# A chunked scan's running sums repeated over the rows by TensorE products, in place of a store to HBM and broadcast loads

## The chip, the cores and the metric

The kernel runs on one core of a Trainium2 chip. A core has five instruction queues: TensorE (PE, matrix products into PSUM), VectorE (DVE), ScalarE (ACT), GpSimd (POOL) and SyncE (SP); SP and POOL issue the DMAs, which 16 DMA engines carry out. The metric is the device time of one execution in microseconds (us), lower is better.

## What is computed

One layer of a hybrid encoder on 1024 rows of width 1024. After a norm and an input projection come three mixers (a window attention "a", a Mamba-2 scan "b", a banded attention "c"), an output projection, a retrieval of 128 experts per row ("PEER": for each row and each of 128 picks, one row of `peer_u` and one of `peer_v`, 4 KB each, chosen by the data), and a gate. The change is inside the scan:

```python
da_cs = jnp.cumsum(dt * a, axis=2)                              # running sums within a chunk, per head
seg = da_cs[:, :, :, None, :] - da_cs[:, :, None, :, :]         # cs[l] - cs[s] for all pairs
decay = jnp.exp(jnp.where(causal, seg, -jnp.inf))
cb = jnp.einsum("bclhn,bcshn->bclsh", cm, bm) * decay
y_diag = jnp.einsum("bclsh,bcshp->bclhp", cb, xdt)
...
ue = jnp.take(expert_u, it, axis=0)                             # PEER, 128 picks per row
ve = jnp.take(expert_v, it, axis=0)
act = jax.nn.gelu(jnp.einsum("td,ted->te", xt, ue), approximate=False) * gt
return jnp.einsum("te,ted->td", act, ve)
```

## The kernel before

**Tiles and groups.** The 1024 rows are 8 tiles of 128 rows (`TILES`), two tiles to a group (`GT = 2`), so 4 groups. The "front" of a group (`front_steps`) is the norm, the projections, the three mixers, the output projection and the second norm; then come the query products of PEER.

**Slots.** PEER runs as 1024 slots and a tail. Slot n gathers one `peer_u` row per token of a tile (POOL, L868, 512 KB) and takes its dot product on DVE (L1575); 44 slots later (`BEHIND`) the matching `peer_v` rows are gathered (L880, 512 KB) and multiplied on PE (L2017). `u_ring` has 6 places and `v_ring` 8: POOL waits for DVE's dots and for PE's products before it gathers into a place again. The front of group 0 runs before the slots (`before_slots`), the fronts of groups 1, 2 and 3 beside them.

**The order.** Every engine runs the same list of steps in order (`whole_program`), each taking its own part of each step. `beside_slots` spreads the steps of a front over the slots 22 to 204, 204 to 456 and 456 to 708 in proportion to the costs in `PACE`; a step without an entry counts 0.2. PSUM has 8 banks; `plan_banks` gives each step the free bank that was used longest ago, out of 8 at first, and out of 4 from slot 25 on, when the other four hold PEER's sums and its normalised rows. PE waits, before it fills a bank, for the copies out of it.

**The scan.** Once per group, step `cs` makes the running sums of 2 tiles x 16 heads: a product with a triangle of ones `tri` gives `cs` with rows on partitions (L1890), a second one gives them transposed (L1891), ACT copies that to `csT` (L1046), and SP stores it to HBM (`cs_rows`, L809, 16 KB). Per tile come, in the order of `scan_steps`: `b_seg`, two `b_turn` (PE transposes L1898, DVE L1440 and L1441), `b_cb` (PE L1904 and L1906, ACT L1083, DVE L1446), two `b_off` (PE L1918, DVE L1454 to L1466), two `b_diag` (PE L1925, DVE L1471), two `b_state` (PE L1932, DVE L1477). In `b_seg`, SP waits until `seg`, which shares memory with the normalised input `uT`, is free (for tile t, the products of `b_diag` of tile t-1, or `z` for a group's first tile) and loads the 16 x 128 running sums of the tile to all 128 partitions (`seg_rows`, L746, 1 MB). ACT makes relu(cs[s] - cs[l]) head by head (L1076, 16 instructions) and one exp over the tile (L1079). DVE's product L1460 in `b_off` needs that exp; ACT's L1083, which DVE's L1446 needs, stands behind it on ACT.

## Time and profile before

| what | us |
|---|---|
| median of 3 runs | 3769.55 |
| lowest, highest | 3768.69, 3770.98 |
| the profiled execution, its own time | 3753.05 |
| its span | 3751.3 |
| PE, DVE, POOL, ACT busy in the span | 2475.1, 2232.2, 1964.5, 765.6 |

The profile is of one execution. Its span runs from the first to the last instruction, and 1.75 us lie around it. An engine counts as busy while it computes, and POOL's rows are the time to issue a gather. The DMA rows say how busy the 16 DMA engines were and what they moved. A wait names the engine and line that waited, and what ended the wait. All engines are well short of 100%, so the shares alone tell no bound; the stretches have to be read one by one.

### The profile page before, as it was taken

How to read it: one execution, taken by the hardware profiler on the slowest of the kernel's cores; microseconds unless marked ns; L12 is line 12 of the kernel's file. 1: busy time of each engine (PE TensorE's matmuls, PEld its weight loads, DVE VectorE, ACT ScalarE, POOL GpSimd, SP SyncE). 2: the span in 40 equal slices, each digit the busy share in tenths (PEclk: the TensorE clock that was granted, in tenths of full speed). 3: DMA queues.
4: the chain of work that ended last, by engine and by line, in shares of the span. 5: the costliest groups of instructions: out<-in, count | busy, mean ns of one | idle time of the engine just before them, and what ended most of it. 6: DMA issues, size and time to landing. Idle time of an engine off the chain costs nothing. (4 is left out here: it accounts for less than half of the span.)

```text
span 3751.3 us, 33795 instructions
## 1 busy us (share of the span) xinstructions
PE 2475.1 (66%) x10840; PEld 1198.8 (32%) x10840; DVE 2232.2 (60%) x5446; ACT 765.6 (20%) x1750; POOL 1964.5 (52%) x2064
## 2 busy tenths in 40 slices
PE   8869688777777758666777767677725534443554
PEld 5644345443333434322333434322301101110111
DVE  2330868566556766675556766776556666666640
ACT  2331222231112222321122222311111111011010
POOL 0000455545555656555555656655656666666663
PEclk9879899778888777778888877778867666766778
DMA  7325899989999999999999999999999999999995
GB/s 229 114 74 188 317 398 385 352 315 355 406 405 404 376 346 390 384 350 406 405 405 403 369 364 384 382 377 407 401 376 381 372 387 382 378 385 377 367 377 202
DMA packets 427462, 1320.09 MB, mean 352 GB/s; under 512 B 54280, under 2 KB 75920, under 8 KB 425112
## 3 DMA queue, kind: packets, MB, share of 16 engines
q0 software_dynamic: 294912, 1073.87, 74.1%
q1 hardware_dynamic: 132376, 244.06, 17.9%
q8 instruction: 89, 1.46, 0.2%
q14 instruction: 85, 0.70, 0.0%
HBM read 1290.69 MB, written 32.60 MB: 353 GB/s over the span
## 5 line engine op out<-in xcount | busy, mean ns | idle before, releaser
L1575 DVE CUSTOM_DVE_ANT_0 u_ring<-u_ring,ps 128x1024 f32<-128x1024 f32 x1024 | 1231.7, 1217 | 551.4 <-DMA u_ring<-peer_u,idx_u 454.5
L868 POOL DMA_INDIRECT u_ring<-peer_u,idx_u x1024 | 981.5, 958 | 960.6 <-DVE idx_u L1553 379.8
L880 POOL DMA_INDIRECT v_ring<-peer_v,idx_v x1024 | 978.4, 955 | 787.1 <-PE ps L2017 340.4
L2017 PE MATMUL ps<-v_ring,spread 128*32 128x512 f32 x4096 | 752.7, 864 | 851.3 <-DMA v_ring<-peer_v,idx_v 744.2
L2017 PEld LDWEIGHTS ps<-v_ring,spread 128*32 128x32 f32 x4096 | 150.8, 138 | 1233.1 <-issue 1231.0
L1754 PE MATMUL ps<-front 128*128 128x512 f32 x1024 | 458.5, 604 | 2.1 <-ACT front L1117 2.1
L1754 PEld LDWEIGHTS ps<-front 128*128 128x128 f32 x1024 | 194.7, 194 | 271.5 <-issue 271.1
L1950 PE MATMUL ps<-front 128*128 128x512 f32 x512 | 232.8, 613 | 13.6 <-DVE front L1491 8.4
L1873 PE MATMUL ps<-front 128*128 128x256 f32 x768 | 197.8, 415 | 1.4 <-issue 1.4
L1873 PEld LDWEIGHTS ps<-front 128*128 128x128 f32 x768 | 156.1, 209 | 58.1 <-issue 34.6
L1950 PEld LDWEIGHTS ps<-front 128*128 128x128 f32 x512 | 98.9, 197 | 151.6 <-issue 151.6
L1382 DVE CUSTOM_DVE_ANT_0 front<-ps,front 128x640 f32<-128x640 f32 (+2 forms) x64 | 42.1, 658 | 154.2 <-PE ps L1841 59.0
L2047 PE MATMUL ps<-front 128*128 128x512 f32 x256 | 123.7, 637 | 13.9 <-issue 10.6
L1404 DVE SCALAR_TENSOR_TENSOR front<-front,taps 128x256 f32<-128x256 f32 x144 | 69.8, 485 | 100.0 <-ACT hist L1026 59.4
L1938 PE MATMUL ps<-front 128*128 128x512 f32 x256 | 120.8, 627 | 1.9 <-issue 1.9
L1841 PE MATMUL ps<-front 64*128 64x128 f32 x480 | 83.9, 328 | 31.9 <-DVE front L1375 9.8
L1851 PE MATMUL ps<-ident,front 128*128 128x128 f32 x240 | 49.0, 334 | 78.5 <-ACT front L1010 68.9
L1865 PE MATMUL ps<-front 128*128 128x64 f32 x480 | 76.7, 305 | 19.0 <-issue 18.6
L1841 PEld LDWEIGHTS ps<-front 64*128 64x128 f32 x480 | 72.1, 228 | 51.4 <-issue 40.0
L1149 ACT ACTIVATE dots<-dots 128x32 f32<-128x32 f32 x32 | 7.3, 229 | 396.9 <-DVE dots L1575 282.9
L1575 DVE DVE_READ_ACCUMULATOR2_ANT dots<- 128x1 f32 x1024 | 84.5, 83 | 0.0
L1865 PEld LDWEIGHTS ps<-front 128*128 128x128 f32 x480 | 70.2, 220 | 39.3 <-issue 36.4
(232 smaller groups left out, 2725.9 us busy)
## 6 DMA issues: line engine op xcount, KB each, us to landing
front<-w_in SPq DMA_DIRECT2D x76, 1024.0 KB
front<-w_out SPq DMA_DIRECT2D x32, 1024.0 KB
front<-peer_w_query SPq DMA_DIRECT2D x32, 1024.0 KB
u_ring<-peer_u,idx_u POOLq DMA_INDIRECT x1024
v_ring<-peer_v,idx_v POOLq DMA_INDIRECT x1024
front<-c_bias_all SPq DMA_DIRECT2D x32, 320.0 KB
front<-x SPq DMA_DIRECT2D x16, 512.0 KB
front<-cs_rows SPq DMA_DIRECT2D x8, 1024.0 KB
```

What stands on the lines that cost most here:

```text
L868: nc.gpsimd.indirect_dma_start(k.u_ring[:, n % RU, :], None, io["peer_u"][0], bass.IndirectOffsetOnAxis(ap=k.idx_u[:, t % 2, j:j + 1], axi ...
L880: nc.gpsimd.indirect_dma_start(row, None, io["peer_v"][0], bass.IndirectOffsetOnAxis(ap=k.idx_v[:, m % 2, column:column + 1], axis=0)).the ...
L1404: ins = stt(a, k.raw[:, c % 2, j:j + NG], k.taps[:, c, j:j + 1], a, ALU.mult, ALU.add)
L1575: nc.vector.tensor_tensor_reduce(out=row, in0=row, in1=k.un_ps, scale=1.0, scalar=0.0, op0=ALU.mult, op1=ALU.add, accum_out=k.dots[:, t % ...
L1754: last = mm(ps, k.uT[:, half * WCH + c, cols(t)], w[:, c, :], start=(half == 0 and c == 0), stop=(half == 1 and c == WCH - 1))
L1841: last = mm(ps[:, n * P:(n + 1) * P], k.qT_c[side, i // 2, cols(t)], k.kT_c[side, i // 2, kt % 6, :], start=True, stop=True)
L1865: last = mm(ps[:, at:at + HD], k.pT[:, no % 2, j, :], k.v_c[:, kt % 6, i * HD:(i + 1) * HD], start=(kt == c_keys(t)[0]), stop=(kt == t))
L1873: last = mm(ps[:, 0:NG], w[j // WCH][:, j % WCH, c % 4 * P:(c % 4 + 1) * P], k.uT[:, j, :], start=(j == 0), stop=(j == DCH - 1))
L1938: last = mm(ps, k.uT[:, c, cols(t)], w[c // WCH][:, c % WCH, :], start=(c == 0), stop=(c == DCH - 1))
L1950: last = mm(ps, k.yT[:, k.o_chunks[part] + j, cols(t)], w[:, j, :], start=(part == 0 and j == 0), stop=(part == 3 and j == WCH - 1))
L2017: last = mm(k.acc_ps[32 * j:32 * j + 32, half * 512:(half + 1) * 512], centres[:, at:at + 32], row[:, half * 512:(half + 1) * 512], start= ...
L2047: last = mm(ps[:, half * 512:(half + 1) * 512], k.fT[:, c, :], k.wg[:, c, half * 512:(half + 1) * 512], start=(c == 0), stop=(c == DCH - 1))
```

## The change

The running sums get to all partitions by products. For each head, PE multiplies the head's column of `dtA` (128 values, repeated 128 times along the free axis by an access pattern of step 0, as the stationary operand) by `tri`; each of the 128 rows of the result is the head's running sum. Four heads fill one PSUM bank, so a tile has 4 such steps (`b_seg` with `part` 0 to 3) with 16 products in all, and ACT's relu reads PSUM in place of SBUF. The second product of `cs`, its copy, the store of `cs_rows` and the eight 1 MB loads go. ACT now makes the waits that SP made before it overwrote `seg`. `b_seg` gets 1.5 in `PACE` for each part, and takes banks in `plan_banks`.

```diff
+SEG = 4
...
-        out += [("b_seg", t)] + halves("b_turn") + [("b_cb", t)] + halves("b_off") + halves("b_diag") + halves("b_state")
+        out += [("b_seg", t, part) for part in range(B_HEADS // SEG)] + halves("b_turn") + [("b_cb", t)] + halves("b_off") + halves("b_diag") + halves("b_state")
...
-            dt=1.8, cs=0.4, z=4.7, y_n=3.0, b_turn=1.2, b_cb=1.0, b_off=0.6, b_diag=3.5, b_state=0.6, y_t=1.2, b_n=4.0, o=4.7, n2=4.0,
+            dt=1.8, cs=0.4, b_seg=1.5, z=4.7, y_n=3.0, b_turn=1.2, b_cb=1.0, b_off=0.6, b_diag=3.5, b_state=0.6, y_t=1.2, b_n=4.0, o=4.7, n2=4.0,
...
-    singles = dict(n1_t=1, sub=1, a_k=GT, a_turn=1, c_turn=1, a_t=1, c_u=1, x=3, z=1, dt=1, cs=5, b_turn=2, b_cb=2, b_off=1, b_diag=1,
+    singles = dict(n1_t=1, sub=1, a_k=GT, a_turn=1, c_turn=1, a_t=1, c_u=1, x=3, z=1, dt=1, cs=4, b_seg=1, b_turn=2, b_cb=2, b_off=1, b_diag=1,
...
-    def seg_rows(t):
-        g, lt = divmod(t, GT)
-        sp.wait_ge(k.cs_out, 16 * (g + 1))
-        filled(("b_diag", t - 1, 1) if lt else ("z", t + GT - 1, 1))
-        src = k.cs_rows[t * B_HEADS:(t + 1) * B_HEADS, :].rearrange("h l -> (h l)")
-        sp.dma_start(k.seg.rearrange("p h l -> p (h l)"), src.partition_broadcast(P)).then_inc(k.seg_in, 16)
...
-        elif kind == "cs":
-            copied(step)
-            sp.dma_start(k.cs_rows[at[0] * GT * B_HEADS:(at[0] + 1) * GT * B_HEADS, :], k.csT[:]).then_inc(k.cs_out, 16)
-        elif kind == "b_seg":
-            seg_rows(*at)
...
-        if g:
-            act.wait_ge(k.cs_out, 16 * g)
         act_fn(k.cs[:], ps[:, 0:n], ACT.Copy).then_inc(copied_, 1)
-        act_fn(k.csT[:], ps[0:n, P:2 * P], ACT.Copy).then_inc(copied_, 1)
...
-    def b_seg(t):
-        act.wait_ge(k.seg_in, 16 * (t + 1))
-        lt = t % GT
-        for hd in range(B_HEADS):
-            at = lt * B_HEADS + hd
-            last = act_fn(k.seg[:, hd, :], k.seg[:, hd, :], ACT.Relu, bias=k.cs[:, at:at + 1], scale=-1.0)
-        last.then_inc(k.seg_rel, 1)
-        act.wait_ge(k.seg_rel, t + 1)
-        act_fn(k.seg, k.seg, ACT.Exp, scale=-1.0).then_inc(k.seg_exp, 1)
+    def b_seg(t, part):
+        _, ps, copied_ = filled(("b_seg", t, part))
+        if part == 0:
+            last = ("b_diag", t - 1, 1) if t % GT else ("z", t + GT - 1, 1)
+            act.wait_ge(k.filled[k.bank[last].place], k.bank[last].n + 1)
+            if t % GT:
+                act.wait_ge(k.m_full, t * B_GROUPS)
+        for i in range(SEG):
+            hd = part * SEG + i
+            at = t % GT * B_HEADS + hd
+            rel = act_fn(k.seg[:, hd, :], ps[:, i * P:(i + 1) * P], ACT.Relu, bias=k.cs[:, at:at + 1], scale=-1.0)
+        rel.then_inc(copied_, 1)
+        if part == B_HEADS // SEG - 1:
+            act.wait_ge(copied_, k.bank["b_seg", t, part].done)
+            act_fn(k.seg, k.seg, ACT.Exp, scale=-1.0).then_inc(k.seg_exp, 1)
...
-        mm(ps[0:n, P:2 * P], k.dtA[:], k.tri[:], start=True, stop=True)
         mm(ps[:, 2 * P:2 * P + n], k.ones[:], k.dtA[:], start=True, stop=True).then_inc(filled, 1)
+
+    def b_seg(t, part):
+
+        pe.wait_ge(k.dtA_full, t // GT + 1)
+        ps, filled = open_(("b_seg", t, part))
+        for i in range(SEG):
+            at = t % GT * B_HEADS + part * SEG + i
+            last = mm(ps[:, i * P:(i + 1) * P], k.dtA[:, at:at + 1].broadcast_to([P, P]), k.tri[:], start=True, stop=True)
+        last.then_inc(filled, 1)
```

The dispatch of PE calls the new `b_seg`. The line numbers of the kernel after are 1 to 13 off those of before.

On PE, in group 0, tile 0 and the start of tile 1, before (L1831 is `y_t`, L1925 `b_diag`, L1932 `b_state`):

```order
L1831 MATMUL ps<-ident,front 128x128 x16
L1898 MATMUL ps<-ident,front 128x128 x8
L1904 MATMUL ps<-ident,front 128x128 x2
L1906 MATMUL ps<-front 128x128 x2
L1918 MATMUL ps<-state,front 128x512 x2
L1925 MATMUL ps<-front 128x64 x16
L1932 MATMUL ps<-front 128x512 x2
L1898 MATMUL ps<-ident,front 128x128 x8
```

The same place after, where L1890 is the new product:

```order
L1822 MATMUL ps<-ident,front 128x128 x16
L1890 MATMUL ps<-tri,dtA 128x128 x16
L1897 MATMUL ps<-ident,front 128x128 x8
L1903 MATMUL ps<-ident,front 128x128 x2
L1905 MATMUL ps<-front 128x128 x2
L1917 MATMUL ps<-state,front 128x512 x2
L1924 MATMUL ps<-front 128x64 x16
L1931 MATMUL ps<-front 128x512 x2
L1890 MATMUL ps<-tri,dtA 128x128 x16
L1897 MATMUL ps<-ident,front 128x128 x8
```

Sixteen products stand ahead of each tile's `b_turn`, and nothing else has moved there.

On PE, in group 1, tile 2 and the start of tile 3, beside the slots (L2017 is the product of four slots' `peer_v` rows), before:

```order
L1831 MATMUL ps<-ident,front 128x128 x4
L1898 MATMUL ps<-ident,front 128x128 x8
L1904 MATMUL ps<-ident,front 128x128 x2
L1906 MATMUL ps<-front 128x128 x2
L1918 MATMUL ps<-state,front 128x512 x2
L2017 MATMUL ps<-v_ring,spread 32x512 x8
L1925 MATMUL ps<-front 128x64 x16
L1932 MATMUL ps<-front 128x512 x2
L1898 MATMUL ps<-ident,front 128x128 x4
```

And after (L2016 is the `peer_v` product, L1985 the turn of its weights):

```order
L1822 MATMUL ps<-ident,front 128x128 x8
L1890 MATMUL ps<-tri,dtA 128x128 x16
L1985 MATMUL ps<-ident,weights 32x32 x4
L2016 MATMUL ps<-v_ring,spread 32x512 x8
L1897 MATMUL ps<-ident,front 128x128 x8
L1903 MATMUL ps<-ident,front 128x128 x2
L1905 MATMUL ps<-front 128x128 x2
L1917 MATMUL ps<-state,front 128x512 x2
L1924 MATMUL ps<-front 128x64 x8
L2016 MATMUL ps<-v_ring,spread 32x512 x8
L1924 MATMUL ps<-front 128x64 x8
L1931 MATMUL ps<-front 128x512 x2
```

The scan of a tile is drawn out: there is one more `peer_v` product within tile 2, and between `b_seg` and `b_turn` stands work of PEER. By the plan, group 1's scan lies in slots 135 to 148 before and 132 to 150 after, group 2's in 358 to 376 and 354 to 379, group 3's in 610 to 628 and 606 to 631.

## Rows read from the trace of the kernel before

**Rows 1.** The page: PE, DVE, ACT, POOL busy; DMA share and GB/s in 40 slices.

```profile
PE 2475.1 (66%) x10840; PEld 1198.8 (32%) x10840; DVE 2232.2 (60%) x5446; ACT 765.6 (20%) x1750; POOL 1964.5 (52%) x2064
DMA  7325899989999999999999999999999999999995
GB/s 229 114 74 188 317 398 385 352 315 355 406 405 404 376 346 390 384 350 406 405 405 403 369 364 384 382 377 407 401 376 381 372 387 382 378 385 377 367 377 202
```

**Rows 2.** The page, DMA queues: POOL's gathers and SP's loads; packets, MB, share.

```profile
q0 software_dynamic: 294912, 1073.87, 74.1%
q1 hardware_dynamic: 132376, 244.06, 17.9%
```

**Rows 3.** The waits, longest in total: us, times, longest.

```profile
PE ps L2017 <- DMA v_ring<-peer_v,idx_v: 744.2, 136, 17.3
...
DVE u_ring L1575 <- DMA u_ring<-peer_u,idx_u: 454.5, 277, 6.0
...
POOL u_ring L868 <- DVE dots L1575: 319.7, 207, 14.2
```

**Rows 4.** Stretches: busy us of PE, PEld, DVE, ACT, POOL, PE clock, DMA share, GB/s.

```profile
0.00:300.00 300.00, 239.02 (x921) 159.01 (x922) 90.96 (x236) 102.82 (x253) 4.67 (x16) 0.86 0.44 143
...
800.00:870.00 70.00, 39.90 (x202) 22.81 (x201) 61.98 (x127) 27.71 (x61) 36.65 (x37) 0.76 0.89 339
1580.00:1680.00 100.00, 63.08 (x279) 29.32 (x277) 84.24 (x183) 23.43 (x49) 60.97 (x63) 0.76 0.92 351
2380.00:2480.00 100.00, 66.01 (x321) 33.80 (x321) 90.09 (x198) 39.45 (x84) 59.91 (x62) 0.67 0.95 366
1680.00:2080.00 400.00, 291.14 (x1193) 127.08 (x1194) 233.08 (x567) 73.58 (x160) 222.87 (x235) 0.85 1.02 402
```

**Rows 5.** ACT's wait for the loads in all, then one load's issue and its relu, tile 3.

```profile
ACT front L1076 <- DMA front<-cs_rows: 70.3, 5, 19.8
...
834.73 0.32 SPq L746 DMA_DIRECT2D front<-cs_rows  x1
...
839.33 4.78 ACT L1076 ACTIVATE front<-front,cs 128x128 f32<-128x128 f32 x16 [14.94 <-DMA front<-cs_rows]
...
846.96 0.41 DVE L1446 TENSOR_TENSOR front<-ps,tri 128x256 f32<-128x256 f32 x1
```

**Rows 6.** Timeline of group 0, tile 0: start, us, engine, line, what.

```profile
228.79 3.30 PE L1831 MATMUL ps<-ident,front 128*128 128x128 f32 x16 [6.51 <-ACT front L1069]
...
230.72 4.79 ACT L1076 ACTIVATE front<-front,cs 128x128 f32<-128x128 f32 x16
...
233.02 0.61 PE L1906 MATMUL ps<-front 128*128 128x128 f32 x4
...
238.63 0.37 ACT L1083 ACTIVATE front<-ps 128x256 f32<-128x256 f32 x1
239.10 0.42 DVE L1446 TENSOR_TENSOR front<-ps,tri 128x256 f32<-128x256 f32 x1 [3.77 <-ACT front L1083]
...
241.91 7.34 PE L1925 MATMUL ps<-front 128*128 128x64 f32 x32 [6.56 <-DVE front L1460]
```

**Rows 7.** Timeline of group 0, tile 1, from the products of tile 0's state.

```profile
249.04 3.43 PE L1932 MATMUL ps<-front 128*128 128x512 f32 x4
...
249.32 0.34 SPq L746 DMA_DIRECT2D front<-cs_rows  x1
...
253.92 4.78 ACT L1076 ACTIVATE front<-front,cs 128x128 f32<-128x128 f32 x16 [14.92 <-DMA front<-cs_rows]
...
258.73 1.91 ACT L1079 ACTIVATE front<-front 128x2048 f32<-128x2048 f32 x1
```

**Rows 8.** Groups by line on ACT: the relu from SBUF, a copy from PSUM; busy, mean ns.

```profile
L1076 ACT ACTIVATE front<-front,cs x128: 384/386/403, 230.7 to 2435.9; 128x128 f32<-128x128 f32 x128
...
L1083 ACT ACTIVATE front<-ps 128x256 f32<-128x256 f32 x8 | 3.0, 375 | 11.8 <-issue 11.8
```

**Rows 9.** SP's load for tile 4, and the pair of gathers around it.

```profile
1543.40 0.54 SPq L746 DMA_DIRECT2D front<-cs_rows  x1
...
1564.59 4.77 ACT L1076 ACTIVATE front<-front,cs 128x128 f32<-128x128 f32 x16
```

More of the change, by code:

```diff
@@ L423, in __init__ @@
         self.whole = sb("whole", [P, HB])
-        self.csT = sb("csT", [HB, P])
         self.ms = sb("ms", [P, 10])
@@ L531, in __init__ @@
         self.scores = dram("scores", (TILES * PH, P, 2 * PK))
-        self.cs_rows = dram("cs_rows", (TILES * B_HEADS, P))
         self.ext_rows = dram("ext_rows", (C_HEADS, C_KEYS + P))
@@ L587, in __init__ @@
          self.raw_full, self.conv_full, self.silu_full, self.dt_soft, self.dt_exp, self.dt_done, self.dtA_full, self.tables_full,
-         self.cs_out, self.seg_in, self.seg_exp, self.seg_rel, self.m_full, self.xend_full, self.off_added, self.state_full,
+         self.seg_exp, self.m_full, self.xend_full, self.off_added, self.state_full,
          self.z_full, self.gated, self.n2_root, self.n2_rs, self.un_full, self.un_here, self.un_kept,
@@ L598, in __init__ @@
             "raw_full conv_full silu_full dt_soft dt_exp dt_done dtA_full tables_full "
-            "cs_out seg_in seg_exp seg_rel m_full xend_full off_added state_full "
+            "seg_exp m_full xend_full off_added state_full "
             "z_full gated n2_root n2_rs un_full un_here un_kept "
@@ L1428, in cs @@
         n = GT * B_HEADS
-        dve.wait_ge(copied_, b.begin + 4)
+        dve.wait_ge(copied_, b.begin + 3)
         tt(k.to_end[:], ps[:, 2 * P:2 * P + n], k.cs[:], ALU.subtract).then_inc(copied_, 1)
@@ L2097, in tensor_program @@
             cs(*at)
+        elif kind == "b_seg":
+            b_seg(*at)
         elif kind == "b_turn":
```

## The prediction

> **What bounds the kernel now.** I read the busy shares first [rows 1]: no engine is over 66%, so none is the bound over the whole. The DMA line under them shows two parts. In the first three to four slices (some 350 us) the DMA engines are 20 to 70% busy: this is the front of group 0, one long chain from engine to engine, in which POOL has nothing to gather yet (4.67 us busy in the first 300 us [rows 4]). Whatever lengthens or shortens that chain moves the end by as much. From slice 5 on the DMA share stands at 9 tenths nearly throughout. The queues say what moves [rows 2]: 1073.87 MB are POOL's gathers, which no edit here touches, and 244.06 MB are SP's loads and stores, to which the loads in question belong. The waits agree [rows 3]: the longest is PE's for the `peer_v` rows (744.2 us), the next DVE's for the `peer_u` rows (454.5 us). Between the scans the engines carry 402 GB/s at a share of 1.02 [rows 4]: saturated. In the three stretches that hold the scans of groups 1 to 3 they carry 339, 351 and 366 GB/s, while DVE is busy 62 of 70, 84 of 100 and 90 of 100 us. There DVE sets the pace: POOL waited 319.7 us in all for dots [rows 3], since a dot stands behind the scan's work in DVE's queue. So there are three regimes: a chain, a DMA bound, and three short DVE bounds.
>
> **Part 1: group 0, in the chain.** The chain goes over ACT: DVE idles 3.77 us for ACT's L1083, which comes right after the exp [rows 6]. Before, the load of tile 0 is hidden: the relu starts at 230.72, right behind ACT's own earlier work, and the 16 take 4.79 us, to 235.5. After, the products stand behind `y_t` (L1831), which ends at 232.1. A product of fp32 is two instructions in the trace: the two of L1906, of the same 128 x 128 x 128, are four rows of 0.61 us together [rows 6], 0.15 us each. Sixteen products are 32 of these, 4.9 us, 1.2 us for a part of four heads, as long as four relus (4.79 / 4). The last part is then full at 237.0 and its relus end at 238.2: 2.7 us later than before. For tile 1 the load was in the open: issued at 249.32, when tile 0's `b_diag` was done, and the relu begins at 253.92 after 14.92 us idle, ending with the exp's start at 258.7 [rows 7]. After, the products follow L1932, which ends at 252.5; the last part is full at 257.4, the relus end at 258.6, 0.1 us earlier. The load's 4.6 us are given back by products that cannot begin until PE has done the state. Together **+2.6 us**. Bounds: L1925, whose 32 instructions took 7.34 us [rows 6], gives 0.23 us each, 7.3 us a tile, if the clock is low there or repeated weights load slowly; tile 0 is then 5.1 us late and tile 1 2.3 us, +7.4. Two thirds of 0.15 would make the relus the limit, about +1. I take 2.6, since L1906 has the very form and stands in the very place.
>
> The ACT relu reads PSUM now, for which no row has this form. From SBUF with a pointer bias it takes 386 ns; a copy of twice the columns from PSUM takes 375 ns [rows 8]. So PSUM as a source is not dear, and I price it at nothing. From 0 to -0.1 us each, the 128 relus are at most 13 us of an engine that is 20% busy [rows 1].
>
> The Trainium skill, ScalarE: Activation LUTs, section What ACT_TABLE_LOAD costs, gives an ACTIVATE with a pointer bias (N + 335) / 1.2 ns and makes no difference by the source. By it the relu from PSUM would be 386 ns too, as the row from SBUF is, and the sum would stay as it is; by the copy's row it would be some 0.1 us less each. No run here shows it yet.
>
> **Part 2: the loads taken out of the saturated part.** Six of the eight loads (tiles 2 to 7) lie beside the slots. One is 1.049 MB, 2.6 us at 402 GB/s. The queue's own average, 17.9% of 3751.3 us for 244.06 MB, is 2.75 us for a MB, 2.9 us a load. If each is saved in full that is 17.3 us. But a load saves time only when the DMA engines are what is waited for. The first of each pair, as at 1543.40 [rows 9], is issued ahead of the scan, where the gathers run at the DMA's rate: three at 2.6 us. The second, as at 834.73 [rows 5], falls into the stretch that DVE sets; I count half, three at 1.3 us. Together **-11.7 us**, bounds 0 and -17.3. The stores and their copies (4 of 16 KB) are nothing against that.
>
> ACT's waits for these loads, 70.3 us in 5 times [rows 5], are no term. Tile 3 shows why: ACT idled 14.94 us until 839.33, and yet DVE's L1446 at 846.96, which needs what ACT does next, came without a wait. DVE had dots and other work in front of it in its queue. The same goes for SP, which no longer waits for `b_diag`: behind L746 on its queue stand a score load, which waits for DVE anyway, and the output weights, which wait for PE.
>
> **Part 3: the order.** `b_seg` now counts 6 per tile instead of 0.2, so a group's scan takes 18 slots in place of 13 (group 1), and 25 in place of 18 (groups 2 and 3), by the plan. That thins DVE's scan work out, in the stretches where DVE is the bound. These lose (402-339)/402 x 70 + (402-351)/402 x 100 + (402-366)/402 x 100 = 11.0 + 12.7 + 9.0 = 32.7 us of DMA time [rows 4]. Most of a stall comes from the two `b_off` next to each other, and these stay near each other, so I let the thinning give back a quarter, 8 us. What the scan gets, the other steps of the front lose: they stand 1 to 5 slots nearer together, and the bank of nearly every later step is another. I put 4 us against it for denser work. Together **-4 us**, bounds -16 (half of the loss) and +8 (no gain, and double the price).
>
> **Part 4: PE's added work beside the slots.** Six tiles at 4.9 us are 29 us, at 7.3 us 44 us. The cover is PE's wait for `peer_v` rows, 744.2 us [rows 3]. The products also stand ahead of `b_turn`, which waits until ACT has emptied a bank of `b_seg`; the plan puts two to three slots between, against 1.2 us for the relus of a bank. **0 us**, bounds 0 and +20; without the cover it is the second rival. The third product of `cs` and its copy that go are 4 each and under 1 us a piece.
>
> **Sum:** +2.6 - 11.7 - 4 + 0 = -13.1 us. Against the profiled execution's own 3753.05 us (its span of 3751.3 and 1.75 around it) that gives 3740. That execution is 16.5 us under the median of the runs; the same difference from the median 3769.55 gives 3756.
>
> **The rivals.**
>
> *The loads were hidden anyway.* In the saturated part the rings may have enough in flight to close a gap of 2.6 us soon after, and the scan's stretches are DVE's. Then at most the three early loads count for half, -3.9 us, the thinning is eaten by the denser rest, and group 0 costs 2.6: -1 us, 3768. For it: ACT's wait for tile 3's load held up nobody [rows 5]. Against it: a share of 1.02 over 400 us [rows 4] leaves no gap to close.
>
> The Trainium skill, DMA: Bandwidth & Descriptors, section Rules for kernel authors, says to issue a DMA early and wait for it late, so that its fixed cost overlaps. That speaks for leaving the even tiles' loads where they were, and by it their removal gives nothing. The trace agrees on the wait (tile 0's relu came with none), not on the bandwidth.
>
> *Slower: the products hold up the `peer_v` products.* PE works in order. In the scan's stretches it is at a granted clock of 0.67 to 0.76 [rows 4], nearer to 1.2 than to 2.4 GHz half of the time, and 63 to 66 of 100 us busy. If a tile's 7.3 us, and the waits for ACT and for a bank of four in rotation, come in front of L2017, the places in `v_ring` come free later, POOL waits, and as it works in order the `peer_u` gathers wait with it. It turns slower where more than some 22 of the 44 us are uncovered: 22 + 2.6 - 11.7 - 4 = +9. With 60% uncovered and no gain from thinning it is +2.6 - 11.7 + 26 = +17; I take +12, 3782. Against it: `v_ring` holds 8 slots, and PE's wait is 744.2 us.
>
> *The whole of it comes.* All six loads in full (-17.3), the thinning gives half of the loss (-16), group 0 +2.6: -31 us, 3739.
>
> **How the numbers follow.** A measurement of this kernel tells about 0.2%, 7.5 us, from no change. Forecast 3756 with chance 0.45; loads hidden 0.25; slower 0.18; the whole 0.12. Faster by over 0.2% is the forecast and the last, less a little for a forecast that comes short: 0.56. Same is 0.26, slower 0.18. The range runs from the whole of it, 3739, to just short of the slower rival's value, 3779: some 1 in 10 lies beyond each end.
>
> **What would show it.** Part 1: in the timeline of group 0, the last relu of tile 0 some 2.7 us later against the end of `y_t`, tile 1's within 1 us of before, the new products at 0.15 us an instruction, and POOL's first gather 2 to 3 us later. Part 2: 8.4 MB less on SP's queue, the rate between the scans still 400 GB/s. Part 3: over 339, 351 and 366 GB/s in the scans' stretches, and less waiting of POOL for dots. Part 4: PE's wait for `peer_v` rows shorter by some 30 us, and POOL's for PE's products not longer. The forecast is wrong if the new products take over 0.23 us an instruction, if the rate in the scans' stretches falls, or if other stretches, with their work nearer together and other banks, lose more than the scans gain.

## The result, and the profile after

| | median us | lowest, highest | runs |
|---|---|---|---|
| before | 3770.22 | 3768.69, 3775.09 | 8 |
| after | 3785.84 | 3780.71, 3801.31 | 8 |

The ratio is 1.0044, 95% interval 1.0026 to 1.0061: the changed kernel is slower by 0.4%, some 16 us, where 3756 us, a gain of 13, was forecast. The profiled execution of after took 3791.66 us (span 3789.9), against 3753.05 of before. That is a difference of 38 us where the medians differ by 16, since single executions of one kernel lie up to some 20 us from their median. So below I compare stretches between two traces, and totals only by medians.

The page of after, to be read against [rows 1, 2]: busy time, DMA share and rate in 40 slices, queues.

```profile
PE 2509.9 (66%) x11088; PEld 1230.3 (32%) x11088; DVE 2233.5 (59%) x5446; ACT 760.6 (20%) x1745; POOL 1959.2 (52%) x2064
DMA  7315999888999999989999999989999999999995
GB/s 227 114 51 186 327 398 356 332 314 328 406 405 403 365 336 395 374 305 404 408 405 404 371 389 382 348 329 406 400 390 379 371 389 374 375 384 381 368 367 197
q0 software_dynamic: 294912, 1073.87, 73.8%
q1 hardware_dynamic: 131032, 235.61, 17.1%
```

SP's queue moves 8.45 MB less, the eight loads and the stores of `cs_rows`. PE has 248 instructions more and is busy 34.8 us longer. No other engine's work has grown. The waits that the prediction named, against [rows 3] (total us, times, longest):

```profile
PE ps L2016 <- DMA v_ring<-peer_v,idx_v: 721.9, 133, 18.3
DVE u_ring L1566 <- DMA u_ring<-peer_u,idx_u: 442.9, 274, 4.9
...
POOL v_ring L868 <- PE ps L2016: 355.3, 104, 17.1
POOL u_ring L856 <- DVE dots L1566: 322.7, 190, 12.3
```

They have hardly moved: PE's wait for the `peer_v` rows is shorter by 22.3 us, POOL's for dots is 3.0 us longer, and POOL's for PE's products is 355.3 us against 340.4. The place of the loss shows when the two traces are cut at the same slots. The stretches that hold the scans of groups 1, 2 and 3 (slots 128 to 156, 346 to 386 and 598 to 640), in before; busy us of PE, PEld, DVE, ACT, POOL, then PE clock, DMA share, GB/s:

```profile
770.00:873.00 103.00, 66.80 (x345) 37.43 (x344) 81.15 (x180) 40.79 (x85) 54.55 (x56) 0.78 0.86 320
1521.00:1652.00 131.00, 76.83 (x403) 39.91 (x404) 103.79 (x233) 42.67 (x91) 78.00 (x80) 0.73 0.93 357
2351.00:2484.00 133.00, 87.44 (x428) 45.84 (x428) 110.46 (x254) 42.65 (x90) 81.32 (x85) 0.70 0.96 369
```

The same slots in after:

```profile
782.00:888.00 106.00, 75.34 (x388) 40.63 (x388) 77.93 (x172) 33.42 (x73) 54.54 (x57) 0.79 0.82 296
1540.00:1678.00 138.00, 88.23 (x428) 47.73 (x420) 100.55 (x222) 32.69 (x78) 76.76 (x81) 0.69 0.89 330
2373.00:2513.00 140.00, 88.81 (x424) 46.05 (x416) 104.75 (x239) 35.05 (x81) 81.19 (x85) 0.68 0.90 337
```

The same slots take 384 us in place of 367, PE is busy 21 us longer, DVE 12 us less, and the DMA engines carry 296, 330 and 337 GB/s in place of 320, 357 and 369. DVE's total busy time is the same (2233.5 against 2232.2), so those 12 us of work have moved out of these slots with the new order. DVE has more idle time in the very stretches in which it had set the pace. Between the scans the rate is as before ([rows 4]: 402):

```profile
1720.00:2100.00 380.00, 284.20 (x1168) 124.35 (x1169) 219.50 (x540) 72.03 (x154) 212.49 (x224) 0.87 1.03 403
```

A second loss of 11 us lies in slots 44 to 128, which hold no step of a scan: 303.5 us in place of 292.5. It is followed up below under the order. A third is in group 0, ahead of the slots, and stands with Part 1 below.

What DVE waited for at the first instruction of `b_turn` in all 16 halves, in before (groups by line: busy us, mean ns, idle time before them and what ended it; "remote" is a release for which the trace shows no instruction):

```profile
L1440 DVE TENSOR_TENSOR front<-ps,dt 128x512 f32<-128x512 f32 x16 | 11.0, 686 | 4.3 <-PE ps L1898 4.2
```

And in after:

```profile
L1431 DVE TENSOR_TENSOR front<-ps,dt 128x512 f32<-128x512 f32 x16 | 11.0, 689 | 44.2 <-PE ps L1897 24.1 <-remote 20.0
```

This wait, 4.3 us before, is 44.2 us now. PE's transposes of `b_turn` stand behind the sixteen products in PE's queue, and behind DVE's `b_turn` stand dots. But the products are not all of it: e2 below, which has the new order and no products, waits 20.1 us there. What a late `b_turn` does to POOL, in the scan of tile 5 in the timeline of after:

```profile
864.35 0.69 DVE L1431 TENSOR_TENSOR front<-ps,dt 128x512 f32<-128x512 f32 x1 [9.66 <-remote]
```

And POOL there:

```profile
867.05 0.94 POOL L856 DMA_INDIRECT u_ring<-peer_u,idx_u  x1 [4.46 <-DVE dots L1566]
```

DVE idled 9.66 us, the dots behind it came late, and POOL waited 4.46 us for a place in `u_ring`. The trace doesn't show what DVE waited for here: PE's transposes had ended at 857.47, 6.9 us before DVE went on.

### The profile page after: what moved, and what is told of

Read it like the earlier page. It is cut to its first block and busy times, and to the rows that moved or that the text cites. A ratio compares the mean times of both kernels' runs of the same rounds, so it can differ in the third digit from the quotient of the medians.

```text
span 3789.9 us, 34303 instructions
## 1 busy us (share of the span) xinstructions
PE 2509.9 (66%) x11088; PEld 1230.3 (32%) x11088; DVE 2233.5 (59%) x5446; ACT 760.6 (20%) x1745; POOL 1959.2 (52%) x2064
## 5 line engine op out<-in xcount | busy, mean ns | idle before, releaser
L868 POOL DMA_INDIRECT v_ring<-peer_v,idx_v x1024 | 975.0, 952 | 818.3 <-PE ps L2016 355.3
L2016 PE MATMUL ps<-v_ring,spread 128*32 128x512 f32 x4096 | 757.2, 870 | 835.3 <-DMA v_ring<-peer_v,idx_v 721.9
L2016 PEld LDWEIGHTS ps<-v_ring,spread 128*32 128x32 f32 x4096 | 151.4, 139 | 1227.0 <-issue 1225.0
L1745 PEld LDWEIGHTS ps<-front 128*128 128x128 f32 x1024 | 193.4, 193 | 265.3 <-issue 264.9
L1864 PE MATMUL ps<-front 128*128 128x256 f32 x768 | 186.8, 398 | 1.8 <-ACT front L986 1.2
L1864 PEld LDWEIGHTS ps<-front 128*128 128x128 f32 x768 | 149.4, 200 | 45.6 <-issue 24.8
L1949 PEld LDWEIGHTS ps<-front 128*128 128x128 f32 x512 | 97.9, 195 | 144.4 <-issue 144.4
L1856 PEld LDWEIGHTS ps<-front 128*128 128x128 f32 x480 | 71.2, 224 | 36.0 <-issue 32.7
L998 ACT ACTIVATE front<-front,c_neg 128x640 f32<-128x640 f32 (+2 forms) x64 | 44.5, 695 | 178.9 <-DVE c_neg L1377 109.7
```

What stands on the lines that cost most here:

```text
L868: nc.gpsimd.indirect_dma_start(row, None, io["peer_v"][0], bass.IndirectOffsetOnAxis(ap=k.idx_v[:, m % 2, column:column + 1], axis=0)).the ...
L1745: last = mm(ps, k.uT[:, half * WCH + c, cols(t)], w[:, c, :], start=(half == 0 and c == 0), stop=(half == 1 and c == WCH - 1))
L1856: last = mm(ps[:, at:at + HD], k.pT[:, no % 2, j, :], k.v_c[:, kt % 6, i * HD:(i + 1) * HD], start=(kt == c_keys(t)[0]), stop=(kt == t))
L1864: last = mm(ps[:, 0:NG], w[j // WCH][:, j % WCH, c % 4 * P:(c % 4 + 1) * P], k.uT[:, j, :], start=(j == 0), stop=(j == DCH - 1))
L1949: last = mm(ps, k.yT[:, k.o_chunks[part] + j, cols(t)], w[:, j, :], start=(part == 0 and j == 0), stop=(part == 3 and j == WCH - 1))
L2016: last = mm(k.acc_ps[32 * j:32 * j + 32, half * 512:(half + 1) * 512], centres[:, at:at + 32], row[:, half * 512:(half + 1) * 512], start= ...
```

## The experiments

The kernels ran in five sets, each on one chip and beside before on the same chip. The chips differ (before: 3778.86, 3657.96, 3760.84, 3759.81 and 3776.98 us), so a kernel is only compared by its ratio to before within its set; the 95% interval stands behind it.

### Products or order: e1, e2, e4 (before 3778.86)

The change does three things: it adds products, drops loads, and moves steps. e1 is the change with the slots of before.

```diff
-            dt=1.8, cs=0.4, b_seg=1.5, z=4.7, ...
+            dt=1.8, cs=0.4, b_seg=0.05, z=4.7, ...
```

> The kernel after with b_seg=0.05 in PACE for each of the four parts, 0.2 a tile as before. Every step then stands in the slot that it had before, and in the bank that it had before but for 9 of 702 in group 0: the products, the relus from PSUM and the missing loads alone are tried. Theory A (the loss of some 15 us is in the order: all other steps of the front moved by 0 to 6 slots): same as before or faster, 3755 to 3770 us. Theory B (the products hold up PE and ACT beside the slots, whatever the order): slower than before by 10 us or more, 3780 and up.

Measured: 3793.79, ratio 1.0040 [1.0021, 1.0060]. The change loses as much in the old slots.

e2 is before with the slots of the change, and e4 before with a third value (2.0); neither changes any work.

```diff
-            dt=1.8, cs=0.4, z=4.7, ...
+            dt=1.8, cs=0.4, b_seg=6.0, z=4.7, ...
```

> The kernel before with b_seg=6.0 in PACE. All other steps stand in the slots and banks that they have in the kernel after (but for 9 banks in group 0); the loads and the old b_seg stay. Theory A: slower than before by what the change lost plus what the products and the missing loads win, 3785 to 3800 us. Theory B: no change, 3765 to 3775.

Measured: 3792.18, ratio 1.0034 [1.0013, 1.0054].

```diff
+            dt=1.8, cs=0.4, b_seg=2.0, z=4.7, ...
```

> The kernel before with b_seg=2.0 in PACE, a third of the shift of the kernel after. If the time hangs smoothly on how much the scan is drawn out, it lies a third of the way from before to the run with 6.0, +5 us with theory A. If each order is its own case (which step falls on which slot and bank), it can come out on either side of before by up to 10 us.

Measured: 3796.78, ratio 1.0041 [1.0022, 1.0060]. The order alone costs 0.3 to 0.4%, and e4, with a third of the shift, costs no less than e2. That is not how a price for density would look, but it fits one step in a bad place. And the two losses, 0.40% in e1 and 0.34% in e2, do not add up: after has both and loses 0.44%.

### The loads alone: e3 (before 3778.86)

```diff
-        sp.dma_start(k.seg.rearrange("p h l -> p (h l)"), src.partition_broadcast(P)).then_inc(k.seg_in, 16)
```

> The kernel before without the eight 1 MB loads: the relus and the exp work on what stands in the memory of seg, so the decay is not computed rightly. Store, waits and order stay. It prices the loads alone. The forecast's part 2 says -11.7 us beside the slots (0 to -17.3), and group 0 loses the load's 4.6 us in the open: some -16 us, 3754. If the loads were hidden by the scan's stretches: -5 us, group 0 alone, 3765.

Measured: 3768.12, ratio 0.9966 [0.9949, 0.9983], that is -12.8 us (3778.86 x 0.0034), group 0's two loads included. Part 2 had -11.7 for the other six alone, and the expectation above -16 for all eight.

### The products and the handshake, apart: r1 to r4 (before 3760.84)

r1 is after and r2 is e1, both again. r3 is r2 with the products made but not read; r4 is r3 without them. Both keep the old slots and have no loads. A first run of r3's kernel, e7, stands in the next set.

> The kernel after, unchanged, beside the next three on one chip, since the ratios of runs on different chips (before: 3779 us on one, 3658 us on another) can't be subtracted. Expected 1.004.

Measured: 3781.68, ratio 1.0054 [1.0031, 1.0077].

> The products in the old order (as e1), with the relus reading them: PE's work, the chain and no loads. If e1's loss holds on this chip, 1.004; this run less r3 is the chain, r3 less r4 is PE's work alone, r4 less 1 is the loads with SP's waits.

Measured: 3776.21, ratio 1.0041 [1.0019, 1.0063].

```diff
-            rel = act_fn(k.seg[:, hd, :], ps[:, i * P:(i + 1) * P], ACT.Relu, bias=k.cs[:, at:at + 1], scale=-1.0)
-        rel.then_inc(copied_, 1)
+            rel = act_fn(k.seg[:, hd, :], k.seg[:, hd, :], ACT.Relu, bias=k.cs[:, at:at + 1], scale=-1.0)
```

> The products in the old order, unused (as e7; the decay is not computed rightly). Theory C (the chain costs, not PE's work): 0.997 to 0.999, at least 0.004 under r2. Theory D: within 0.002 of r2.

Measured: 3773.50, ratio 1.0034 [1.0013, 1.0056].

```diff
-            last = mm(ps[:, i * P:(i + 1) * P], k.dtA[:, at:at + 1].broadcast_to([P, P]), k.tri[:], start=True, stop=True)
-        last.then_inc(filled, 1)
```

> As r3, with the products left out of it too: the old order, no loads, no products, SP's waits for b_diag and cs gone (the decay is not computed rightly). e3, which kept those waits, came to 0.9966. Expected 0.996 to 0.998; theory C puts r3 within 0.001 of it, theory D 0.005 above.

Measured: 3750.23, ratio 0.9971 [0.9949, 0.9994].

This splits the change: the loads are worth -0.29% (r4), the products on PE, which nobody reads, +0.63% (r4 to r3, 23.3 us by the medians), the chain from product over relu to exp +0.07% (r3 to r2), and the order +0.13% (r2 to r1). Only the second of these steps stands well clear of the noise. The loads' is just clear of it (0.9949 to 0.9994), the last two are inside it. The second is the term that the forecast had at nothing.

The traces of r4 and r3 show how it comes about, in the scan of tile 5. In r4, PE's transposes follow the last copies of tile 4 at once (timeline of PE; L1890 is the transpose here):

```profile
836.12 0.63 PE L1890 MATMUL ps<-ident,front 128*128 128x128 f32 x4 [1.67 <-DVE front L1460]
836.68 1.92 PE L2009 MATMUL ps<-v_ring,spread 128*32 128x512 f32 x16
839.35 0.63 PE L1890 MATMUL ps<-ident,front 128*128 128x128 f32 x4 [0.75 <-DVE front L1460]
```

and DVE's `b_turn` starts without a wait:

```profile
841.45 0.68 DVE L1429 TENSOR_TENSOR front<-ps,dt 128x512 f32<-128x512 f32 x1
```

In r3 the products (L1888) take those places:

```profile
841.57 1.13 PE L1888 MATMUL ps<-tri,dtA 128*128 128x128 f32 x8 [1.66 <-DVE front L1460]
844.80 5.21 PE L1888 MATMUL ps<-tri,dtA 128*128 128x128 f32 x24 [2.10 <-DVE front L1460]
849.85 0.60 PE L1895 MATMUL ps<-ident,front 128*128 128x128 f32 x4
```

and DVE waits:

```profile
851.11 0.69 DVE L1429 TENSOR_TENSOR front<-ps,dt 128x512 f32<-128x512 f32 x1 [4.13 <-PE ps L1895]
```

Both are released by the same DVE instruction, L1460 (`b_diag`), which frees the bank. In r4 the first transpose starts 0.83 us after L1460's start (836.12 against 835.29). In r3 it starts 9.1 us after it (849.85 against 840.74), because the second group of products waits for the second L1460 and then takes 5.21 us. The last of DVE's work on tile 4 does not fill that. The products are slow there: 24 instructions in 5.21 us are 0.217 us each, with a granted clock of 0.54, and the eight before them 1.13 us, 0.141 us each, at 0.93. The stretches of r3 (columns as above):

```profile
841.50:843.00 1.50, 1.13 (x8) 0.97 (x8) 1.47 (x6) 1.47 (x2) 1.20 (x2) 0.93 0.78 238
844.80:850.00 5.20, 5.20 (x26) 5.20 (x27) 2.18 (x4) 0.00 (x0) 3.75 (x4) 0.54 0.93 315
```

The first is near the upper of the clock's two levels, 2.4 GHz, and the second near the lower, 1.2. PE had idled 1.66 us before the first and 2.10 us before the second. Over all halves DVE waited, in r4:

```profile
L1429 DVE TENSOR_TENSOR front<-ps,dt 128x512 f32<-128x512 f32 x16 | 11.0, 686 | 6.7 <-PE ps L1890 3.9 <-remote 2.7
```

and in r3:

```profile
L1429 DVE TENSOR_TENSOR front<-ps,dt 128x512 f32<-128x512 f32 x16 | 11.0, 688 | 34.1 <-PE ps L1895 17.4 <-remote 16.6
```

27.4 us more of waiting, beside a loss of 23.3 by the medians. Of the 34.1 us, 6.5 are in group 0, and the three waits marked "remote" (16.6 us) went on for 1.7 to 7.6 us after PE's transposes had ended. So PE's queue accounts for about half of this wait as far as the trace shows, and what ended the rest is open. (The two profiled executions are only 1.6 us apart, one above its median and one below, so the spans say nothing here.) The time of the three scan stretches together (cut by slots as above) sorts the kernels by what they do:

| slots and products | us in the three stretches |
|---|---|
| no products, slots of before: before, e3, r4, s3 | 367.9, 365.0, 363.1, 369.8 |
| no products, other slots: e2, e4 | 370.4, 373.2 |
| products, slots of before: e1, r2, r3, t1 | 384.8, 383.2, 379.4, 385.2 |
| products, slots of the change: after, r1, s2, t2 | 383.1, 378.0, 372.9, 374.2 |
| the faster chip of the next set: e6 (no products, slots of before), e7, e8 (products, slots of before), e5 (products, slots of the change) | 362.0, 364.6, 364.1, 350.4 |

In the slots of before, products cost these stretches 16 us (r4 to r3) and 20 us (e3 to e1). In the slots of the change it is 5 us by the means of these rows, and on the faster chip 3 us (e6 to e7), each from a few single executions. So the price seems to hang on the slots and on the chip.

### The order's part: early c_bias (before 3657.96, a faster chip)

Where do e2 and e4 lose? Slots 98 to 104 took 22.6 us in before, 22.7 in e1 and 22.9 in e3, but 33.9 in after, 31.9 in e2 and 29.3 in e4. There DVE waits for a load of group 1's attention bias (`c_bias`). Its issue on SP and DVE's wait, in before:

```profile
672.14 20.36 SPq L646 DMA_DIRECT2D front<-c_bias_all  x4
...
680.78 0.56 DVE L1382 CUSTOM_DVE_ANT_0 front<-ps,front 128x384 f32<-128x384 f32 x1 [2.76 <-DMA front<-c_bias_all]
```

The same two in after:

```profile
671.75 17.69 SPq L646 DMA_DIRECT2D front<-c_bias_all  x3
...
687.68 0.56 DVE L1373 CUSTOM_DVE_ANT_0 front<-ps,front 128x384 f32<-128x384 f32 x1 [11.77 <-DMA front<-c_bias_all]
```

The load is issued at the same time, behind two loads of `w_in`; the first step that needs it stands at slot 96 by the change's plan and at 98 before. DVE waits 11.77 us in place of 2.76, r1 12.1 and e4 13.4, and e2 shows the same without any product:

```profile
681.76 0.56 DVE L1382 CUSTOM_DVE_ANT_0 front<-ps,front 128x384 f32<-128x384 f32 x1 [11.95 <-DMA front<-c_bias_all]
```

But before has the same wait too, in groups 2 and 3:

```profile
1389.11 0.82 DVE L1382 CUSTOM_DVE_ANT_0 front<-ps,front 128x640 f32<-128x640 f32 x1 [12.34 <-DMA front<-c_bias_all]
...
2218.43 0.82 DVE L1382 CUSTOM_DVE_ANT_0 front<-ps,front 128x640 f32<-128x640 f32 x1 [12.50 <-DMA front<-c_bias_all]
```

Over the whole span DVE waits 34.8 us for `c_bias` in before, 32.0 in after, 42.9 in r1, 38.6 in e2 and 23.8 in e4. So group 1's wait is longer in each of these traces of another order, but the total isn't in all of them, and that this one wait is what the order costs is argued, not shown.

The next kernels put the first two `c_bias` loads of each group a few steps forward, ahead of the tenth of the twelve `x` steps (the expectation of e5 says ninth).

```diff
-    out += projected_steps(g) + blend(a_steps(g), x_steps(g)) + [("x_silu", g), ("c_bias", g, 0), ("c_bias", g, 1)]
+    mixed = blend(a_steps(g), x_steps(g))
+    at = max(mixed.index(("x", g, XCH - 3)), mixed.index(("a_s", g * GT + GT - 1, A_PAIRS - 1)) + 1)
+    mixed[at:at] = [("c_bias", g, 0), ("c_bias", g, 1)]
+    out += projected_steps(g) + mixed + [("x_silu", g)]
```

e5 is after with this edit, e6 before with it.

> The kernel after, with the first two c_bias loads of a group issued ahead of the ninth of its twelve x steps rather than behind the last one, where two 1 MB weight loads stand in front of them on SP's queue. In the new order DVE waited 11.8 us for that load in group 1 (slots 98 to 104), in the old one 2.8 us. Theory A (that wait is what the new order costs): some 10 us less than the kernel after in group 1 and perhaps as much in groups 2 and 3, so 1.000 of before or less. If the wait only moves on: within 3 us of the kernel after, 1.004.

Measured: 3628.80, ratio 0.9929 [0.9916, 0.9942].

> The kernel before with the same early c_bias loads. Its DVE waited only 2.8 us there. Theory A: at most 3 us a group faster, 0.998 to 1.000. If the early load helps as much here as in the new order, then it is no property of the new order: 0.997 or less.

Measured: 3630.19, ratio 0.9923 [0.9910, 0.9936].

e7 is r3's kernel on this chip, and e8 is e5 in the old slots with the parts of `b_seg` and the other steps mixed.

```diff
-        out += [("b_seg", t, part) for part in range(B_HEADS // SEG)] + halves("b_turn") + [("b_cb", t)] + ...
+        out += [seg[0], turn[0], seg[1], turn[1], seg[2], ("b_cb", t), seg[3]] + ...
```

> The products in the old order, as in e1, but nobody waits for them and nobody reads them: the relus work on what stands in the memory of seg (the decay is not computed rightly), and the banks of b_seg need no copy. It holds PE's added work alone; e1 holds the chain PE to ACT to PE as well. e3 (no loads, no products) came to 0.9966, e1 to 1.0040. Theory C (the chain costs: b_turn stands behind ACT's relus, ACT behind PE): near e3, 0.997 to 0.999. Theory D (PE's work alone costs): near e1, 1.003 to 1.005.

Measured: 3661.26, ratio 1.0006 [0.9996, 1.0015]; r3, the same kernel, has 1.0034 [1.0013, 1.0056]. The intervals barely meet. In e7's trace DVE waits 14.3 us for the `c_bias` load of group 1, in the old slots, and 47.5 us for `c_bias` in all, so on this chip the old order has that wait too.

> The kernel after with the old pace (b_seg=0.05 a part), the early c_bias loads, and the parts of b_seg between the steps behind them: part 0, b_turn 0, part 1, b_turn 1, part 2, b_cb, part 3. DVE has the work of b_turn and b_cb while the parts are filled and emptied. Theory C: it wins back most of what e1 lost in the scans (20 us), so 0.997 to 1.000, and could beat before. Theory D: as e1, 1.003 or more.

Measured: 3631.64, ratio 0.9930 [0.9916, 0.9944], the same as e5. DVE's wait at `b_turn` fell from e5's 22.3 to 10.6 us, 5.4 us appeared where it waits for the exp and 2.2 at `b_off`; the time didn't move. Since e8 also went back to the old slots, two things differ between it and e5.

So the early load gains more than was at stake, in before too, where it removes the waits of groups 2 and 3 as well: DVE's wait for `c_bias` is 6.2 us in all in e6, none in s3 and 1.9 in e5. With it the change costs 0.06% on this chip, which can't be told from nothing.

### A repair of the place, and the early load again: s1 to s4 (before 3759.81)

If the transposes suffer for standing behind the products, the products can stand behind the transposes. s1 is that, in the old slots.

```diff
-        out += [("b_seg", t, part) for part in range(B_HEADS // SEG)] + halves("b_turn") + [("b_cb", t)] + halves("b_off") + ...
+        seg = [("b_seg", t, part) for part in range(B_HEADS // SEG)]
+        out += halves("b_turn") + [("b_cb", t)] + seg + halves("b_off") + ...
```

> The kernel after in the old pace (as r2), with the four parts of b_seg behind b_turn and b_cb in scan_steps. Same products, same amount of work on PE. If the place in PE's queue costs (DVE waits for the transposes behind the products): DVE's wait at b_turn falls from 34.6 us to under 10, and the time to 0.998 to 1.000 of before, 0.004 to 0.006 under r2. If it is the amount of work: 1.003 to 1.005, as r2. It can also move on to DVE's wait for the exp in b_off, 1.001 to 1.003.

Measured: 3794.76, ratio 1.0096 [1.0064, 1.0128]. This is the slowest of all against before, and the theory that the place ahead of `b_turn` is the fault fell with it. The groups by line on DVE in s1: the sum with the exp's tile (L1452), the first instruction of `b_off` (L1446):

```profile
L1452 DVE TENSOR_TENSOR front<-front 128x1024 f32<-128x1024 f32 x16 | 19.6, 1224 | 17.2 <-ACT front L1071 17.2
...
L1446 DVE TENSOR_TENSOR front<-ps,from_start 128x512 f32<-128x512 f32 x16 | 11.0, 688 | 31.3 <-PE ps L1918 25.0 <-issue 6.3
```

The wait at `b_turn` is gone (0.3 us), and 31.3 us stand one step later, at PE's product for `b_off`, which is now the one behind the sixteen products; 17.2 us for the exp are added, which had no wait in r2. The scan stretches take 398.6 us. The scan is a chain of short steps that alternate between PE and DVE, and in the two places tried sixteen products in one block hold up the step that follows them.

s2 and s3 are e5 and e6 on this chip, s4 is s1 with the early load.

> The kernel after with the early c_bias loads (as e5), beside s3 and s4 on one chip. The new order's own loss gone: s2 less s3 is then products (+0.0063) and loads taken out (-0.003) alone, +0.002 to +0.004. If the order costs by itself, +0.006 or more.

Measured: 3752.93, ratio 0.9976 [0.9955, 0.9998].

> The kernel before with the early c_bias loads (as e6): 0.990 to 0.994.

Measured: 3743.90, ratio 0.9961 [0.9936, 0.9985].

> s1 with the early c_bias loads. If both repairs hold and add up: 0.002 to 0.004 under s3, 0.987 to 0.991. If the products cost wherever they stand: at or above s3.

Measured: 3770.64, ratio 1.0025 [1.0001, 1.0048].

s4 is 0.64% above s3, so with the products behind `b_turn` the early load doesn't hide them. With them in the change's own place it costs 0.15% (s2 to s3, hardly more than the noise) in place of 0.54% on a chip of the same speed (r1). Before gains by the early load on both chips (0.9961 here, 0.9923 in e6); the kernel after itself ran on neither.

### Is the wider spread worth anything: t1, t2 (before 3776.98)

Part 3 said that drawing the scan out helps, and the `c_bias` wait might have hidden it. t1 and t2 both have the early load and the products; t1 has the slots of before, t2 (which is s2) those of the change.

```diff
-            dt=1.8, cs=0.4, b_seg=1.5, z=4.7, ...
+            dt=1.8, cs=0.4, b_seg=0.05, z=4.7, ...
```

> The change whole, with the steps in the slots of before (b_seg at 0.05 in PACE) and the two c_bias loads moved forward; beside it runs the same with the change's own slots. Asked is what the slots of the change are worth once VectorE's wait for the c_bias load is out. Theory 1, the slots cost time by that wait alone: this is then faster than the other or equal to it, 0.998 of before, the other 0.998. Theory 2, the thinning of the scan does give back what the forecast's Part 3 said (8 us), and the wait hid it: this is slower than the other by some 0.2%, 1.000 of before, about what the products alone cost (0.63%) less the loads (0.3%) and the early loads (0.4%). Theory 3, the slots cost by other work nearer together as well: this is 0.996 and faster than the other by over 0.1%.

Measured: 3770.68, ratio 0.9984 [0.9963, 1.0005].

> The changed kernel with the two c_bias loads moved forward, a second time, as the partner of the run with the slots of before. Expected 0.9976 of before again, with 0.996 to 0.999 as bounds.

Measured: 3766.69, ratio 0.9984 [0.9966, 1.0002].

No difference. In the scans the wider spread does give back: those stretches take 385.2 us in t1 and 374.2 in t2, and t2's DVE waits 30.6 us at `b_turn` against 33.0. The totals differ by 4.0 us by the medians, inside their noise, so where t2 loses what it gained there isn't shown.

## Why the prediction was wrong

**What bounds the kernel** was read rightly: most of the products' cost lies where DVE sets the pace (16 of 23 us from r4 to r3) and 3 us of it in group 0's chain, and the rate of the saturated stretches didn't change.

**Part 1, group 0 (+2.6): the mechanism held, the whole cost was 4.2.** The timeline of after, against [rows 6, 7]; tile 0 first:

```profile
226.95 3.31 PE L1822 MATMUL ps<-ident,front 128*128 128x128 f32 x16 [6.51 <-ACT front L1054]
230.09 3.74 PE L1890 MATMUL ps<-tri,dtA 128*128 128x128 f32 x32
...
231.19 4.24 ACT L1066 ACTIVATE front<-ps,cs 128x128 f32<-128x128 f32 x16 [2.46 <-PE ps L1890]
...
238.56 0.37 ACT L1074 ACTIVATE front<-ps 128x256 f32<-128x256 f32 x1
```

Tile 1, where PE's L1931 (`b_state` of tile 0) ended at 252.70, at 248.97 + 3.73:

```profile
248.97 3.73 PE L1931 MATMUL ps<-front 128*128 128x512 f32 x4
252.49 4.29 PE L1890 MATMUL ps<-tri,dtA 128*128 128x128 f32 x32
...
254.13 4.25 ACT L1066 ACTIVATE front<-ps,cs 128x128 f32<-128x128 f32 x16 [15.21 <-PE ps L1890]
258.41 1.91 ACT L1070 ACTIVATE front<-front 128x2048 f32<-128x2048 f32 x1
```

An instruction of the product took 0.117 us (3.74 / 32), where 0.15 was taken, so the relus were the limit. From the end of `y_t` to ACT's copy of `b_cb` it is 8.3 us (230.26 to 238.56) against 6.54 (232.09 to 238.63): 1.8 us later, where 2.7 was said. In tile 1 the exp starts 258.41, 5.71 us after PE's L1931 ended (252.70), against 6.26: 0.5 us earlier, where 0.1 was said. Together +1.2 up to there. But the front of group 0 as a whole lost more. POOL's first gather, in before and in after:

```profile
385.65 1.09 POOL L868 DMA_INDIRECT u_ring<-peer_u,idx_u  x1 [379.82 <-DVE idx_u L1553]
...
388.01 1.09 POOL L856 DMA_INDIRECT u_ring<-peer_u,idx_u  x1 [382.19 <-DVE idx_u L1544]
```

From the end of `y_t` to it are 153.6 us in before (385.65 - 232.09) and 157.8 in after (388.01 - 230.26): +4.2, 1.6 more than forecast. (Counted from the start of each span it is 2.4 us later, as `y_t` happened to end 1.8 us earlier.) The other traces say the same: 153.4 to 154.2 with the loads and no products (e2, e4, e6, s3), and 157.3 to 158.4 with products that are read (e1, e5, r1, r2, s1, s2, s4, t1, t2; e8 alone has 154.1). Without loads and products it is 150.6 and 150.7 (e3, r4), with products that nobody reads 153.8 and 154.0 (r3, e7). So the loads taken out give 2.9 us there, PE's work costs 3.2, and the relus' waiting for it 4.3. Some 1.9 us of the 4.2 come behind the scan, in the output projection. Its first 2.5 us or so in before and in after (columns as above):

```profile
287.50:290.00 2.50, 2.45 (x6) 1.25 (x7) 0.00 (x0) 0.00 (x0) 0.00 (x0) 1.00 0.63 159
...
287.30:290.00 2.70, 2.64 (x3) 1.18 (x4) 0.00 (x0) 0.00 (x0) 0.00 (x0) 0.50 0.66 185
```

It begins at the lower level of the clock in after and at the upper one in before, though PE was busy for 2.6 and 2.7 of the 11 us from 272 to 283; why isn't shown. The step of this part that fell short is that it ended at the scan. That PSUM as a source costs a relu nothing came true, and a little more: the trace of after gives shortest, median and longest of

```profile
L1066 ACT ACTIVATE front<-ps,cs x128: 347/377/480, 231.2 to 2476.1; 128x128 f32<-128x128 f32 x128
```

377 ns against 386 from SBUF [rows 8], and 0.265 us from one to the next (4.24 / 16) against 0.30. The Trainium skill, ScalarE: Activation LUTs, section What ACT_TABLE_LOAD costs, gives one formula for an ACTIVATE with a pointer bias and names no source; here the median differs by 9 ns and the measurement decides, though nothing of the result hangs on it.

**Part 2, the loads (-11.7): about right.** e3 gave -12.8, r4 -10.9 (3760.84 x 0.0029), for all eight loads. Less the 2.9 us of group 0 that leaves -8 to -10 for the six that the term priced, well inside its bounds, with 6 to 8 us of noise either way. Whether half is the right share where DVE sets the pace isn't tested by itself. The rival that the loads were hidden anyway would have given e3 -5 us, and its interval (-6 to -19 us) leaves that out.

**Part 3, the order (-4): wrong in sign.** What failed is the sentence that put 4 us against "denser work". At least a part of the price isn't spread over the front: one step of group 1, two slots earlier, met a load whose issue did not move in time, and DVE waited 9.0 us longer (11.77 against 2.76). The plan's list of slots and the trace of before, where DVE already waited 2.76 us for that load at that place and over 12 us in groups 2 and 3, would have shown it. That it is the whole price isn't shown, since DVE's total wait for `c_bias` didn't grow in after; t1 and t2, in which that wait is gone and the two orders take the same time, speak for it. The thinning itself did help the scans (t1, t2), but gave nothing over the whole. By r1 and r2 the order cost +0.13%, by e2 +0.34%, with intervals of 0.2% either way; its bound of +8 us holds for the first, not for the second.

**Part 4, PE's added work beside the slots (0): the step that failed.** The work was sized well: in r3 the products are busy 39.3 us over eight tiles, 4.9 a tile, the value taken. The cover was the error. PE's wait for `peer_v` rows is a sum over the whole span, most of it where the scan isn't (28 of 760.6 us in r3's three scan stretches); it says nothing of the moment at which the products stand. There PE is in a chain with DVE, in which each waits for the other in turn. The prediction said that PE is busy 63 to 66 of 100 us there, and saw `b_turn` behind the products, but priced only the wait for a bank. Measured are +23.3 us (r4 to r3), of which 3.2 are group 0's; the 20 that are left are the upper bound of this term, where nothing was taken. By the medians of r1 to r4 the change is -10.6 for the loads, +23.3 for the products, +2.7 for the chain (group 0's 4.3 alone would be more than that) and +5.5 for the order, +20.8 together; the first two carry it, and the forecast had only the first.

**The slower rival** had the sign and nearly the size (+12 against +16 us). Its way was `v_ring`: the `peer_v` products behind the new ones come late, and POOL waits for them. That can be seen beside the way over DVE's `b_turn`, which it hadn't. In the scan of tile 5 PE's L2009 starts 1.4 us after DVE's L1460 in r4 (836.68 against 835.29), and the same product, L2014, 9.6 us after it in r3 (850.38 against 840.74). Both traces have a gather of POOL that waited 6.09 us for a dot (832.20 in r4, 837.64 in r3). The fifth `peer_v` gather after it, in r4 and in r3:

```profile
844.34 0.94 POOL L868 DMA_INDIRECT v_ring<-peer_v,idx_v  x1 [0.30 <-issue]
...
852.60 0.94 POOL L868 DMA_INDIRECT v_ring<-peer_v,idx_v  x1 [3.11 <-PE ps L2014]
```

Over the three scan stretches POOL waited 28.8 us for PE's products in r3 and 19.0 in r4, and 70.7 for DVE's dots against 64.5. So both ways took part, and no run tells them apart. The size is in part luck, since the rival priced group 0 at 2.6 and the order at -4.

**What stays open.** e8 halved DVE's wait at `b_turn` and s1 removed it, and neither gained, so that wait is a place at which the loss shows, not a price that can be taken off by itself. The products cost 0.63% on one chip (r3 against r4); on the faster one r3's kernel is at 1.0006, and r4's didn't run there, so what they cost there isn't measured. Releases marked "remote" make up 16.6 of the 34.1 us of r3, mostly after PE's transposes had ended; the trace doesn't name them. And why the change costs less with the `c_bias` loads early (0.15 and 0.06%) than without (0.54%) isn't settled: the chips differ, and the order's wait is only one candidate.

## What to carry to other kernels

A long total wait of an engine is cover only for work that falls where the engine waits. Before work is put into an in-order queue, read the timeline at that very place, and price what stands behind it on this engine and on the engine that waits for it: here 16 small products per tile, 39 us in all of an engine that idles a third of the time, cost 23 on one chip, and moving them one place further on cost more. When a planner's cost of one step changes, compare the slots of the steps that first need a load with the time at which that load is issued: two slots made one wait 9 us longer, and moving the load gained 0.4 to 0.8% in the kernel before, which had such waits already.

## What the runs showed of the hardware that was not expected

The stationary operand made by an access pattern of step 0 loads as fast as another one. The trace of after, the new product's load and that of an ordinary product (L1905, `b_cb`), shortest, median, longest of one in ns:

```profile
L1890 PEld LDWEIGHTS ps<-tri,dtA x256: 185/190/338, 230.0 to 2461.2; 128*128 128x128 f32 x128
...
L1905 PEld LDWEIGHTS ps<-front x32: 190/192/333, 234.7 to 2477.2; 128*128 128x128 f32 x32
```

The same instruction costs 0.117 us each in group 0's chain at a granted clock of 1.00 and 0.217 beside the slots at 0.54, so a price read in one stage isn't that of another. And moving two loads per group forward gained 0.39% on one chip and 0.77% on another (s3, e6), more than the whole change was thought to bring. The Trainium skill, DMA: Bandwidth & Descriptors, section Rules for kernel authors, says to issue a DMA early and wait for it late. The prediction used that rule for the loads of `cs_rows`; these runs agree with it for the loads of `c_bias`, for which DVE stood idle for 34.8 us in before and not at all in s3.
